# An expert's count of further blocks loaded behind its gate and up products, two trims of the prologue, and a shorter VectorE list

## The reference

```python
mod = silu(c) @ ada_w + ada_b                  # 1024 x 6144: shift, scale and gate of both sub-layers
u = x * (1 + scale1) + shift1
k, v, q, lru_in, gelu_in, gate_a, gate_b = split(u @ w_in)
ya = sliding_window_attention(q, k, v, rel_bias, sink)   # window 128, one learned sink per head
   # m = max(logits.max(), sink); p = exp(logits - m); probs = p / (p.sum() + exp(sink - m))
a = exp(-8 * sigmoid(r) * softplus(-lambda))             # RG-LRU, after a causal convolution of width 4
h = scan(a, sqrt(1 - a*a) * (i * xc)); yb = h * gelu(gelu_in)
x1 = layer_norm(ALPHA*x + gate1 * ((sigmoid(gate_a)*ya + sigmoid(gate_b)*yb) @ w_out))
u2 = x1 * (1 + scale2) + shift2
# router: softmax over 16 experts, one group of 4 experts, then the top 2 of it for each token
y = sum_e w_e * ((silu(u2 @ w_gate[e]) * (u2 @ w_up[e])) @ w_down[e])   # each w 1024x512 or 512x1024
out = layer_norm(ALPHA*x1 + gate2 * y)
```

## Time and profile before

| | |
|---|---|
| median of 3 runs | 754.45 us (753.3 to 755.13) |
| profiled execution, its own time | 755.41 us |
| its span in the trace | 753.3 us |
| mean granted clock of TensorE | 0.946 of full |
| PE busy | 652.9 us, 87% of the span |
| DVE, ACT, POOL busy | 352.4, 226.9, 98.7 us |
| moved by DMA | 189.41 MB, 251 GB/s over the span |

### The profile page before, as it was taken

The page is one execution under the profiler, slowest core; times in us unless marked ns, Lnnn a source line. Parts: engine busy times, 40 slices in busy tenths (PEclk is TensorE's granted clock), DMA queues, the critical chain, the costliest instruction groups (busy, mean ns, idle before and its releaser), DMA issues.

```text
span 753.3 us, 15566 instructions
## 1 busy us (share of the span) xinstructions
PE 652.9 (87%) x6011; PEld 430.4 (57%) x6012; DVE 352.4 (47%) x691; ACT 226.9 (30%) x471; POOL 98.7 (13%) x185
## 2 busy tenths in 40 slices
PE   0799999998989799999999659799999999999910
PEld 0276666676767577777788445355555555555500
DVE  0265444378888786666756673211111111111117
ACT  0233533557554454555600401001111111111112
POOL 0131001110000000000000012122222222222240
PEclk9999999999999899999999858899999999999965
DMA  9999766293211222223692899999999999991156
GB/s 300 374 323 308 260 224 228 90 329 101 85 57 56 85 85 82 59 61 104 218 422 118 328 411 358 418 419 416 421 418 418 418 419 418 417 372 42 42 141 215
DMA packets 83924, 189.41 MB, mean 251 GB/s; under 512 B 7432, under 2 KB 60008, under 8 KB 68528
## 3 DMA queue, kind: packets, MB, share of 16 engines
q1 hardware_dynamic: 67664, 148.66, 52.3%
q0 software_dynamic: 7376, 32.26, 12.5%
q10 hardware_dynamic: 8848, 8.01, 3.2%
HBM read 174.83 MB, written 14.07 MB: 251 GB/s over the span
## 4 chain that ended last, share of the span: by engine, by line
PE 67%; DVE 11%; DMA 9%; ACT 5%; issue 5%; SPq 2%; POOL 1%; ACTq 0%; POOLq 0%; DVEq 0%
PE psum L1488 20%; PE psum L1499 10%; DMA raw<-in_w_in_dram 7%; PE psum L1290 7%; PE psum L1292 6%; PE psum L1291 6%; PE psum L1478 2%; PE psum L1471 2%; PE psum L1411 2%; PE psum L1413 2%; PE psum L1412 2%; PE psum L1256 2%; SPq L396 1%; PE psum L1333 1%; ACT ssb L731 1%
## 5 line engine op out<-in xcount | busy, mean ns | idle before, releaser
L1488 PE MATMUL psum<-wg,xs 128*32 128x256 f32 x1280 | 150.7, 390 | 0.5 <-ACT xs L791 0.5
L1488 PE MATMUL psum<-wu,xs 128*32 128x256 f32 x1280 | 150.8, 390 | 0.0
L1290 PE MATMUL psum<-uh,whi 128*128 128x512 f32 x336 | 138.3, 412 | 0.1
L1291 PE MATMUL psum<-ul,whi 128*128 128x512 f32 x336 | 132.0, 393 | 0.0
L1292 PE MATMUL psum<-uh,wlo 128*128 128x512 f32 x336 | 132.0, 393 | 0.0
L1488 PEld LDWEIGHTS psum<-wg,xs 128*32 128x32 f32 x1280 | 72.6, 112 | 53.9 <-issue 5.2
L785 ACT ACTIVATE hsil<-psum 64x256 f32<-64x256 f32 x40 | 15.0, 376 | 230.9 <-PE psum L1488 230.9
L864 DVE TENSOR_TENSOR wlo<-raw,whi 128x1024 fp32r<-128x1024 f32 x42 | 51.4, 1224 | 68.4 <-ACT whi L615 68.3
L1171 DVE TENSOR_TENSOR h_sb<-psum,hsil 64x256 f32<-64x256 f32 x40 | 17.1, 428 | 139.4 <-ACT hsil L785 139.4
L1499 PE MATMUL psum<-wd,hT 128*32 128x256 f32 x1280 | 77.4, 382 | 1.1 <-DVE hT L1177 1.1
L1290 PEld LDWEIGHTS psum<-uh,whi 128*128 128x128 f32 x336 | 63.8, 190 | 21.1 <-issue 7.6
(11 more groups left out here) (252 smaller groups left out, 832.6 us busy)
## 6 DMA issues: line engine op xcount, KB each, us to landing
wg<-in_moe_w_gate_dram SPq DMA_DIRECT2D x32, 1024.0 KB
wu<-in_moe_w_up_dram SPq DMA_DIRECT2D x32, 1024.0 KB
wd<-in_moe_w_down_dram SPq DMA_DIRECT2D x32, 1024.0 KB
raw<-in_w_in_dram SPq DMA_DIRECT2D x42, 512.0 KB, 3.9
ada<-in_ada_w_dram POOLq DMA_DIRECT2D x16, 1024.0 KB, 7.0
ada<-in_ada_w_dram SPq DMA_DIRECT2D x8, 1024.0 KB, 17.0
y_d<-ysb ACTq DMA_DIRECT2D x160, 32.0 KB
y_d<-zrow POOLq DMA_DIRECT2D x8, 512.0 KB, 6.5
```

What stands on the lines that cost most here:

```text
L1290: mmul(bank[s % 2], h[:, k, :], uh[:, k, :], start=(k == 0), stop=False)
L1291: mmul(bank[s % 2], h[:, k, :], ul[:, k, :], start=False, stop=False)
L1488: ins = mmul(psum[32 * g:32 * g + 32, 0, 0:256], xs[:, k % 2, k // 2, :], wgu[slot][g // 2][:, k, (g % 2) * 256:(g % 2) * 256 + 256], star ...
```

## The change

PE: `more` is loaded behind `gate_up(first)`. Prologue: the identity is loaded ahead of the other constants, with its own semaphore; `adab1` is set to zero by DVE and its four groups come as single rows (8 KB in all) with a semaphore of their own; PE's two small products stand behind piece j = 6 of the modulation; DVE's two operations on lambda stand behind `cact`; SP starts x and tile 0 in turn. DVE's list: the sink is kept negated, so one operation takes the place of two for each attention unit; the squares a² move to ACT; the GeLU's constant goes into ACT's square as a scale, and its `+1` into the multiplication.

```diff
@@ PE @@
                     first = pe.value_load(ctrl[0:1, bass.ds(3 * trip + (FIRST + n + 1), 1)], min_val=1, max_val=NBLK - 1)
-                    more = pe.value_load(ctrl[0:1, bass.ds(3 * trip + (MORE + n + 1), 1)], min_val=0, max_val=NOVER)
                     landed = trip * 32 + (64 if slot == 0 else 32)
                     h_transpose(first - 1)
                     gate_up(first, slot, landed)
+                    more = pe.value_load(ctrl[0:1, bass.ds(3 * trip + (MORE + n + 1), 1)], min_val=0, max_val=NOVER)
                     x_transpose(first + 1)
@@ PE, prologue @@
-            pe.wait_ge(const_in, 16)
-            pe.wait_ge(param_in, 16 * 9)
-            nc.tensor.transpose(bank[7][:, 0:64], prm[:, :], ident[0:64, 0:64]).then_inc(S["pcol_ps"], 1)
-            pe.wait_ge(S["setup_done"], 5)
-            pe.wait_ge(S["pool_in"], 16 * 2)
-            mmul(psum[0:NQ, 6, 0:384], rbs[:, :], cst[0:NBUCKET + 1, C_HOT:C_HOT + 384], start=True, stop=True)\
-                .then_inc(S["bvec_ps"], 1)
...
             for j in range(8):
                 pe.wait_ge(ada1_sem[j], 16)
                 modulate(j, ada1[:, j, :], bank[4], S["mod1_ps"])
+                if j == 6:
+                    pe.wait_ge(id_in, 16)
+                    pe.wait_ge(param_in, 16 * 5)
+                    nc.tensor.transpose(bank[7][:, 0:64], prm[:, :], ident[0:64, 0:64]).then_inc(S["pcol_ps"], 1)
+                    pe.wait_ge(S["setup_done"], 6)
+                    pe.wait_ge(S["pool_in"], 16 * 2)
+                    pe.wait_ge(const_in, 16)
+                    mmul(psum[0:NQ, 6, 0:384], rbs[:, :], cst[0:NBUCKET + 1, C_HOT:C_HOT + 384], start=True, stop=True)\
+                        .then_inc(S["bvec_ps"], 1)
@@ SP @@
-            for t in range(3):
-                load_tile(t)
+            load_x(0)
+            load_tile(0)
+            load_x(1)
+            load_tile(1)
+            load_tile(2)
@@ ACT, its DMAs @@
-            act.dma_start(cst[:, :], consts[:, 0:C_END]).then_inc(const_in, 16)
+            act.dma_start(cst[:, C_ID:C_ID + P], consts[:, C_ID:C_ID + P]).then_inc(id_in, 16)
+            act.wait_ge(S["setup_done"], 6)
+            for g in range(4):
+                act.dma_start(adab1[32 * g:32 * g + 1, :], ada_b[0, g * 512:(g + 1) * 512].rearrange("(a n) -> a n", a=1))\
+                    .then_inc(adab_in, 16)
...
-            for g in range(4):
-                act.dma_start(adab1[32 * g:32 * g + 32, :], ada_b[0, g * 512:(g + 1) * 512].partition_broadcast(32))\
-                    .then_inc(param_in, 16)
+            act.dma_start(cst[:, P:C_END], consts[:, P:C_END]).then_inc(const_in, 16)
@@ ACT @@
-                    A(gt[i % 2][:, :], b, ACT.Square).then_inc(S["sq_done"], 1)
+                    A(gt[i % 2][:, :], b, ACT.Square, scale=math.sqrt(0.044715)).then_inc(S["sq_done"], 1)
...
+                for i in {14: (0, 1), 15: (2, 3, 4), 16: (5, 6, 7)}.get(s, ()):
+                    act.wait_ge(S["ta_done"], i + 1)
+                    if i >= 2:
+                        act.wait_ge(S["m2_done"], i - 1)
+                    A(tt[i % 2][:, :], dec[:, i, :], ACT.Square).then_inc(S["a2_done"], 1)
@@ DVE @@
+            V.memset(adab1[:, :], 0.0).then_inc(S["setup_done"], 1)
...
                     chain(V.tensor_reduce(mx[:, r, :].rearrange("p (a b) -> p a b", a=2), sl, AX.X, ALU.max))
-                    chain(V.tensor_tensor(mx[:, r, :], mx[:, r, :], sinkp[:, 4 * hg:4 * hg + 4], ALU.max))
-                    k_ = mark(V.tensor_scalar(negm[:, r, :], mx[:, r, :], -1.0, None, ALU.mult))
-                    dve.wait_ge(S["dve_order"], k_)
-                    V.tensor_tensor(sm[:, r, :], sinkp[:, 4 * hg:4 * hg + 4], mx[:, r, :], ALU.subtract)\
+                    chain(V.scalar_tensor_tensor(negm[:, r, :], mx[:, r, :], -1.0, nsink[:, 4 * hg:4 * hg + 4],
+                                                 ALU.mult, ALU.min))
+                    V.tensor_tensor(sm[:, r, :], negm[:, r, :], nsink[:, 4 * hg:4 * hg + 4], ALU.subtract)\
                         .then_inc(S["logit_done"], 1)
...
-                        dve.wait_ge(S["ta_done"], i + 1)
-                        k_ = mark(V.tensor_tensor(tt[i % 2][:, :], dec[:, i, :], dec[:, i, :], ALU.mult))
-                        dve.wait_ge(S["dve_order"], k_)
+                        dve.wait_ge(S["a2_done"], i + 1)
...
-                    chain(V.tensor_scalar(gt[i % 2][:, :], gt[i % 2][:, :], 0.044715, 1.0, ALU.mult, ALU.add))
                     dve.wait_ge(S["evac"], AT["lg", i] + 1)
-                    V.tensor_tensor(gt[i % 2][:, :], gt[i % 2][:, :], xg[i % 2][:, :], ALU.mult).then_inc(S["g_arg"], 1)
+                    V.scalar_tensor_tensor(gt[i % 2][:, :], gt[i % 2][:, :], 1.0, xg[i % 2][:, :], ALU.add, ALU.mult)\
+                        .then_inc(S["g_arg"], 1)
```

More of the change, by code:

```diff
@@ L162, in hybrid_layer @@
         mod1 = small("mod1", [P, 16])
-        sinkp = small("sinkp", [P, NQ])
+        nsink = small("nsink", [P, NQ])
         mx = small("mx", [P, 4, 4])
@@ L339, in sem @@
             return ctx.enter_context(nc.semaphore(name))
-        const_in, param_in, small_in = (sem(n) for n in ("const_in", "param_in", "small_in"))
+        id_in, const_in, param_in, adab_in, small_in = (sem(n) for n in ("id_in", "const_in", "param_in", "adab_in", "small_in"))
         x_in = [sem(f"x_in{c}") for c in range(2)]
@@ L367, in hybrid_layer @@
             fin_z fin_s fin_sqrt xT_m_ps xgs_rdy xs_rdy gu_ps silu_done h_done_m
-            hT_ps hT_sb d_ps y_ev fin_n fin_out v_ps v_sb idn_done pool_in t_done""".split()
+            hT_ps hT_sb d_ps y_ev fin_n fin_out v_ps v_sb idn_done pool_in t_done a2_done""".split()
         S = {n: sem(n) for n in names}
@@ L394, in _, with load_x @@
             x_v = x[0].rearrange("(t p) n -> p t n", p=P)
-            for q in range(2):
+            def load_x(q):
                 sp.dma_start(x_sb[:, :, 512 * q:512 * q + 512], x_v[:, :, 512 * q:512 * q + 512]).then_inc(x_in[q], 16)
@@ L602, in _ @@
             A(pcol[:, :], bank[7][:, 0:64], ACT.Copy).then_inc(S["pcol_sb"], 1)
-            act.wait_ge(S["dve_order"], 2)
+            act.wait_ge(S["dve_order"], 4)
             A(tiny[:, 1, :], tiny[:, 1, :], ACT.Exp).then_inc(S["exp_small"], 1)
@@ L848, in _ @@
             V.memset(epst[:, :], EPS).then_inc(S["setup_done"], 1)
-            dve.wait_ge(S["pcol_sb"], 1)
-            lam = pcol[:, 56:64]
-            chain(V.tensor_scalar(tiny[:, 2, :], lam, -1.0, None, ALU.mult))
-            chain(V.tensor_tensor(tiny[:, 1, :], tiny[:, 2, :], lam, ALU.min))
             dve.wait_ge(S["exp_small"], 1)
@@ L857, in _ @@
             dve.wait_ge(S["c_done"], 1)
+            dve.wait_ge(S["pcol_sb"], 1)
+            lam = pcol[:, 56:64]
+            chain(V.tensor_scalar(tiny[:, 2, :], lam, -1.0, None, ALU.mult))
+            chain(V.tensor_tensor(tiny[:, 1, :], tiny[:, 2, :], lam, ALU.min))
             def split(t):
@@ L869, in split @@
                         .then_inc(S["split_lo"], 1)
-            dve.wait_ge(param_in, 16 * 9)
+            dve.wait_ge(adab_in, 16 * 4)
             dve.wait_ge(S["mod1_ps"], 8)
@@ L913, in _ @@
             mark(V.tensor_scalar(nk8[:, :], tiny[:, 5, :], -LRU_C, None, ALU.mult))
-            dve.wait_ge(S["setup_done"], 5)
+            dve.wait_ge(S["setup_done"], 6)
             dve.wait_ge(S["pool_in"], 16 * 2)
-            chain(V.tensor_copy(sinkp[:, :].rearrange("p (g a b) -> p g a b", g=4, a=2),
-                                sinkt[:, :].rearrange("p (g b a) -> p g a b", g=4, a=2)))
+            chain(V.tensor_scalar(nsink[:, :].rearrange("p (g a b) -> p g a b", g=4, a=2),
+                                  sinkt[:, :].rearrange("p (g b a) -> p g a b", g=4, a=2), -1.0, None, ALU.mult))
             for s in range(NPROJ + 2):
```

## The result

| | before | after |
|---|---|---|
| median | 755.34 us (752.64 to 756.92, 20 runs) | 751.11 us (747.33 to 754.38, 20 runs) |
| profiled execution, its span | 755.41, 753.3 | 748.59, 746.5 |
| mean granted clock | 0.946 | 0.952 |

The ratio is 0.9943 (95% interval 0.9929 to 0.9957), or −4.3 us (−5.4 to −3.2): faster by 0.6%, and inside the range of 743.5 to 752.8. Forecast were −5.7. The profiled execution is the third fastest of its 20, 2.5 us under their median, so its trace shows 6.8 us less, more than the change is worth; the experiments show where that came from.

What follows compares the result with a forecast made beforehand. Tile loads through full DMA engines were taken to bound the prologue, DVE and ACT the mixing, PE's switches and then weights the experts. −0.7 − 4.1 − 0.9 = −5.7 on 755.41 gives 749.7; 0.96 over median, so 748.8 us, range 743.5 to 752.8.

Steps and rivals of the forecast that it cites:

- part 1: Prologue: fewer bytes in a full DMA stretch bring tile 3's landing forward; −0.7 us, bounds −1.6 to +1.0.
- part 2: Mixing, DVE's shorter list: the chain up to 253.80 shortens by 2.6 + 0.6 + 0.9 = 4.1 us, bounds 2.6 to 6.0.
- part 3: Experts' switches: −1.2 kept up to expert 12, +2.0 for the clock, −1.7 after; −0.9 us, bounds −8.2 to +1.5.
- Brings nothing by itself: Prologue: PE's start at about 8 us gains nothing alone, since ada1's last piece lands at 28.3.
- 0.6 to 0.85 us: Prologue: time for 0.25 MB less in a full stretch, at the 292 to 420 GB/s seen.
- I take 0.9 us for this: Mixing: gain from moving DVE's squares ahead of the square root to ACT, 0.9 us out of 3.7.
- Rival B: Mixing: ACT takes over from DVE, squares delay exponentials and copies, stalls stay; part 2 about −1, time 751.9; chance 0.12.
- L718's counterpart: Mixing: PE's product at step 17 waits up to 2.8 us near 181 for ACT's copy L718, costing nothing.
- gross of 8.2: Experts: idle time saved at switches before waits for weights, 6.5 us up to expert 12 and 1.7 from 13 to 15.
- Rival A: Experts: weights do not bind, expert 12's land in time; part 3 is −8.2, time 741.5; chance 0.12.
- Rival C: Experts' loop: instruction pages fetched at more turns, each 3.0 us and 2.4 of clock; time 761; chance 0.04.
- Rival D: Experts: moved load not hidden, `x_transpose` 0.4 us later at 15 switches; −2 for part 3, time 747.7; chance 0.07.

Runs made afterwards that it cites:

- c_only: The kernel before with only the hunks of DVE's list, squares on ACT included: 752.74 us, ratio 0.9959 to before.
- again: The changed kernel run once more, unaltered, for a second trace: 753.83 us (one time).
- early_gelu: `early` with DVE's multiplication for the GeLU put ahead of its split of a tile and its scan: 738.02 us, ratio 0.9764 to before.
- gelu_back: The changed kernel with only the GeLU's operation (0.044715 g*g + 1) put back on DVE: 755.72 us (one time).
- b_only: The kernel before with only the hunks of the prologue: 753.88 us, ratio 0.997 to before.
- a_only: The kernel before with only PE's load of `more` moved behind `gate_up`: 754.63 us, ratio 0.9987 to before.
- less_before: The kernel before with a quarter of the down weights of experts 3 to 15 not loaded: 754.70 us, ratio 0.9991 to before.
- early: The changed kernel with the squares on DVE, three pairs of operations ahead of step 15's split of a tile: 746.72 us, ratio 0.988 to before.

## Why the prediction was right, term by term

The direction, the range and the likeliest case held. The sum (−5.7) was 1.4 too large in size against −4.3 (−5.4 to −3.2), and its terms were less good than their sum: by the marks of the traces part 1 gave 0.6 more than forecast, part 2 1.7 less and part 3 0.5 less. That the errors partly cancelled was luck.

**Part 1, −0.7.** The path went on over tile 3 as forecast: PE waits for its split in eight of nine traces with the new prologue and in three of four with the old one. "Brings nothing by itself" is not quite so: in `c_only` the split was done at 60.30 and PE, without any idle time, came at 60.55, so there PE's own pace was the limit. In four traces with the old prologue P is 59.96 to 61.01, mean 60.4; in nine with the new one 58.27 to 60.12, mean 59.1: −1.3, within the bound of −1.6, though single traces of the two groups overlap. The step that fell short was "0.6 to 0.85 us" from bytes alone: the same full DMA engines moved 424 GB/s in place of 350 from 10 to 20 us, and the last piece of ada_w landed 2.3 us earlier. Which load did that, and why 1.3 of it is left at tile 3, stays open. The wait forecast at 1 to 2.5 us ahead of P was 0.00 to 2.94. The bound on the other side, a fall of the clock at tile 3, happened in `again` and `early_gelu`.

**Part 2, −4.1.** The term for the chain behind the square root, 2.6 + 0.6 = 3.2, measured 3.40 (73.46 to 70.06); `gelu_back` puts 2.8 of it on the GeLU and leaves 0.6 for the sink. The term "I take 0.9 us for this" had the wrong sign: the squares on ACT cost 1.0 (S − P). ACT was taken to be idle enough before the second copy; but the six squares and their waits for the two buffers took 5.1 us, where 4.1 were idle. Rival B named this mechanism, and was right on the squares and wrong on the rest. Net −2.4. The new wait for L718's counterpart came as forecast, at 183.19 to 184.39, 1.2 us, and cost nothing.

**Part 3, −0.9.** The order of events is as forecast: no idle time at the switches in a trip, waits at experts 11 and 12, transfer rate unchanged. Sizes: waits of 6.0 at the two experts, forecast 5.3; kept up to expert 12 are 0.2 us, forecast 1.2, since the weights landed later than the 1.4 us allowed behind their count, and the slack was not there. Half clock behind the wait: in six of seven traces with the whole load of weights and the moved `value_load` 3.4 us of it, worth 1.7 (forecast 2.0), and none in the first one. Over all traces D − G is 266.3 on average in those seven (264.56 to 267.57) and 266.7 in the five without part A: −0.4, which such a spread does not tell from 0. The gross of 8.2 was nearly right: 7.3 in the pair with fewer bytes. Of the missing 0.9, 0.76 was booked for expert 3, whose stall did not get shorter: 2.65 to 4.61 us with the load moved, 3.31 to 4.65 without.

**The rest.** −1.3 − 2.4 − 0.4 = −4.1, against −4.3 measured. The first profiled pair differs by 6.8 because the clock fell behind the wait in other executions and not in that one, because its stall at expert 3 was 2.65 us, the shortest of all, and because 0.9 us less lie behind D. Rival A is out: it needed slack that the queue does not have, and only with 8% of the bytes away did its time (741.5, measured 743.2) come. Rival C: the changed kernel has one long "issue" wait, at expert 3, as before; the only other is 0.32 us at expert 4. Rival D: no wait appeared ahead of `x_transpose`. The rates in slices 26 to 36 stayed at 417 to 422 GB/s. That is under the figure of about 435 of the Trainium skill ("Perfetto Trace Analysis", Roofline), and the trace agrees with it as a ceiling: this kernel comes near and does not reach it.

## What to carry to other kernels

Before a saving on the busiest engine is booked, count the bytes that it needs by then: an engine with no wait for data in the trace can still be within one or two microseconds of one, and the wait then mostly costs the clock as well. Bytes alone do not price a transfer: with 0.25 MB of small copies gone and the constants moved back, DMA engines that were full either way moved 0.74 MB more in 10 us. Work that is moved from a loaded to a less loaded engine must be placed in that engine's idle time, not only on it; here the same squares cost 1 us on ACT, and gained 3.3 on DVE once done while both engines waited for a tile. When an engine waits in a chain at every step for one short operation, look first at what stands ahead of that operation on its engine: moving one instruction in DVE's list gave 8.7 us, twice what all three parts of the change did.

## What the runs showed of the hardware

The length of an idle time of TensorE did not tell whether the clock would fall behind it. Behind 3.52 to 3.57 us at expert 12 it was at half for 3.4 us in six traces and stayed full in one. In the changed kernel it fell behind 2.05 us at 171 us, and behind 1.80 at 221 it did not. In `c_only` it stayed full behind 2.72 us and fell behind 1.82 (0.83 over 10 us):

```profile
186.11 0.44 PE L1335 MATMUL psum<-ptb,vv 128*64 128x256 f32 x2 [2.72 <-ACT q_sb L723]
...
224.09 0.44 PE L1335 MATMUL psum<-ptb,vv 128*64 128x256 f32 x2 [1.82 <-ACT ptb L680]
```
```profile
186.00:200.00 14.00, 13.89 (x72) 11.02 (x72) 9.61 (x21) 10.14 (x26) 0.00 (x0) 1.00 0.15 46
224.00:234.00 10.00, 9.90 (x44) 7.07 (x44) 8.77 (x13) 4.84 (x8) 0.00 (x0) 0.83 0.18 52
```

What a fall costs depends on whose the chain is. Where PE was on it, behind tile 3, ahead of the experts and behind expert 12, some 3.4 us more at half cost 1.4 to 2.0 us, so that two traces of one kernel can differ by that much at each such place. Between S and W, where the chain is ACT's and DVE's, it cost nothing: W − S is 73.44 to 73.46 with 3.4 us at half (the kernel before, `b_only`) as with 6.8 (`a_only`, `less_before`), and 70.06 to 70.08 with none (`early`) as with 3.4 (`c_only`).

The begin of the fourth projection moved by up to 1.9 us between executions with the same prologue (58.27 to 60.12 in nine traces), with full DMA engines ahead of it (share 1.02 in 40 to 60 us before). A change of under 1 us in such a stretch can't be read from one pair of traces.
